# A split-precision transformer kernel whose matmul operands get other start addresses in SBUF

## The reference

```python
# first block
h = rmsnorm(x, g[0]);  proj = h @ w_in            # pool, conv, gates, q, k, v, index parts
y_pool, y_conv, y_attn = pool_mixer(..), conv_mixer(..), sparse_attention(..)
up = einsum('bsnc,ncd->bsnd', branches, w_branch)
gates = sigmoid(h @ w_gate + b_gate)
x = x + rmsnorm(sum(gates * up) @ w_out, g[1])
h = rmsnorm(x, g[2])
x = x + rmsnorm(square(relu(h @ w_up)) @ w_down, g[3])
# second block
shift, scale, gate = split(silu(c) @ w_ada + b_ada, 3)
h, hc = modulate(rmsnorm(x, norm_g), ..), modulate(rmsnorm(ctx, norm_g), ..)
p = h @ w_in_2                                    # q, k, v, z_a, u_b, z_b, g_a, g_b
attn = attention(rope(q), [rope(k), kc], [v, vc]) # kc, vc from hc @ w_in_2
y = (sigmoid(g_a) * (attn * silu(z_a)) @ w_pa + sigmoid(g_b) * (fft(u_b) * silu(z_b)) @ w_pb) @ w_o
out = rmsnorm(x + gate * y, final_g)
```

## Time and profile before

| | |
|---|---|
| median of the runs | 2207.93 us |
| span of the profiled execution | 2206.3 us |
| around the span, median less span | 1.6 us |
| TensorE busy, matmuls | 2197.4 us, 16122 instructions |
| VectorE busy | 1509.1 us |
| ScalarE busy | 1066.9 us |
| read from HBM | 468.30 MB |
| mean granted TensorE clock | 0.999 of 2.4 GHz |

### The profile page before, as it was taken

How to read it: one execution, slowest core, us unless ns; L and a number is a source line. 1 busy time by engine, 2 the same in 40 slices (tenths; PEclk the granted TensorE clock), 3 DMA queues, 4 the chain that set the end, 5 groups by cost and what they waited for, 6 DMA issues and landing times.

```text
span 2206.3 us, 37987 instructions
## 1 busy us (share of the span) xinstructions
PE 2197.4 (100%) x16122; PEld 2068.7 (94%) x16122; DVE 1509.1 (68%) x1910; ACT 1066.9 (48%) x1418; POOL 63.1 (3%) x72
## 2 busy tenths in 40 slices
PE   9999999999999999999999999999999999999998
PEld 9999999999999889989988988998889999999987
DVE  7789588888889657544554555555766656577776
ACT  5444445544444546444443543444656555444443
POOL 1000000000000000000000000000100000010001
PEclk9999999999999999999999999999999999999999
DMA  8876676788787755656656666656664445678784
GB/s 275 241 225 209 192 247 221 228 281 258 256 278 264 241 182 182 195 194 194 192 195 195 183 202 203 197 186 207 235 196 148 135 144 172 216 264 294 251 281 156
DMA packets 248034, 475.00 MB, mean 215 GB/s; under 512 B 21526, under 2 KB 26000, under 8 KB 247096
## 3 DMA queue, kind: packets, MB, share of 16 engines
q1 hardware_dynamic: 243032, 454.40, 64.7%
q0 software_dynamic: 4832, 18.16, 2.5%
HBM read 468.30 MB, written 5.78 MB: 215 GB/s over the span
## 4 chain that ended last, share of the span: by engine, by line
PE 99%; issue 0%; DVE 0%; ACT 0%; POOLq 0%; POOL 0%; DVEq 0%
PE ps L888 21%; PE ps L889 21%; PE ps L890 21%; PE ps L881 11%; PE ps L882 11%; PE ps L883 11%; PE ps L805 1%; PE ps L705 1%; PE ps L794 0%; PE ps L674 0%; PE ps L902 0%; PE ps L717 0%; PE ps L784 0%; PE ps L785 0%; PE ps L783 0%
## 5 line engine op out<-in xcount | busy, mean ns | idle before, releaser
L888 PE MATMUL ps<-op0h,whiW 128*128 128x256 f32 x3376 | 936.8, 277 | 0.0
L890 PE MATMUL ps<-op0h,wloW 128*128 128x256 f32 x3376 | 932.3, 276 | 0.0
L889 PE MATMUL ps<-op0l,whiW 128*128 128x256 f32 x3376 | 932.2, 276 | 0.0
L1279 DVE TENSOR_TENSOR wloW<-raw,whiW 128x1024 fp32r<-128x1024 f32 (+1 forms) x503 | 611.0, 1227 | 339.0 <-ACT whiW L935 336.9
L935 ACT ACTIVATE whiW<-raw 128x1024 fp32r<-128x1024 f32 (+1 forms) x504 | 529.0, 1058 | 581.1 <-PE ps L890 482.8
L888 PEld LDWEIGHTS ps<-op0h,whiW 128*128 128x128 f32 x3376 | 633.7, 188 | 2.2 <-issue 1.6
L889 PEld LDWEIGHTS ps<-op0l,whiW 128*128 128x128 f32 x3376 | 633.8, 188 | 0.5
L890 PEld LDWEIGHTS ps<-op0h,wloW 128*128 128x128 f32 x3376 | 633.7, 188 | 0.0
L1279 DVE TENSOR_TENSOR wloT<-raw,whiT 128x1024 fp32r<-128x1024 f32 (+1 forms) x264 | 317.4, 1211 | 249.5 <-ACT whiT L935 248.0
L935 ACT ACTIVATE whiT<-raw 128x1024 fp32r<-128x1024 f32 (+1 forms) x264 | 273.7, 1046 | 291.0 <-PE ps L883 243.0
L881 PE MATMUL ps<-whiT,op1h 128*128 128x512 f32 x640 | 249.2, 389 | 0.0
(11 more groups left out here) (308 smaller groups left out, 2070.2 us busy)
## 6 DMA issues: line engine op xcount, KB each, us to landing
raw<-in_w_in SPq DMA_DIRECT2D x256, 512.0 KB, 4.4
raw<-in_w_up SPq DMA_DIRECT2D x128, 512.0 KB, 3.7
raw<-in_w_down SPq DMA_DIRECT2D x128, 512.0 KB, 4.0
raw<-in_w_ada SPq DMA_DIRECT2D x96, 512.0 KB, 4.7
raw<-in_w_gate SPq DMA_DIRECT2D x96, 512.0 KB, 4.8
raw<-in_w_out SPq DMA_DIRECT2D x64, 512.0 KB, 5.1
raw<-in_w_branch SPq DMA_DIRECT2D x48, 512.0 KB, 4.9
raw<-in_w_proj_a SPq DMA_DIRECT2D x24, 512.0 KB, 5.7
```

The lines of the kernel that those rows point to most:

```text
L888: pe.matmul(o, wh, xh[:, ka, :], start=first and m % 2 == 0, stop=False, skip_group_check=True)
L889: pe.matmul(o, wh, xl[:, ka, :], start=False, stop=False, skip_group_check=True)
L890: mm = pe.matmul(o, wl, xh[:, ka, :], start=False, stop=last, skip_group_check=True)
L1279: v.tensor_tensor(wlo[job.mode][q % NSPL][:, :, 0:job.n], x, h.bitcast(F32), ALU.subtract).then_inc(s_lo, 1)
```

## The change

The places of the operands in SBUF change, and nothing else. The high part of chunk `q` begins at `PLACES[q // 4 % 16]` bytes past its buffer's base, the low part at `PLACES[(q // 4 * 3 + 5) % 16]`, in both modes; bases are 0 modulo 256 (`o - 64`). The operands x0, x1, x2, pool, conv, mix and hid0 to hid3 get tiles of their own (`placed`), which begin 0, 64, 4, 32, 32, 8, 4, 68, 64 and 12 bytes past the place where `op0h` or `op1h` begins; the low part lies 16384 bytes behind the high part. att and four stay at the start of `op1h`, and ya, ctx and mg where they are. The buffers are some bytes longer, and what is allocated after them moves up. The tmp tiles and `ident` go from 64 to 0 modulo 256 by that; `big` is put at 64 modulo 256 again. The lines where an operand's tile is written or read name the placed tile instead of `op0h`, `op0l`, `op1h`, `op1l`.

```diff
--- before.py
+++ after.py
@@ -22,6 +22,7 @@
 ATT_SCALE = 128 ** -0.5
 BIG = 1e30
 SKEW = 128 * 513 + 384
+PLACES = dict(zip("abcdefghijklmnop", (0, 64, 128, 192, 4, 68, 132, 196, 8, 72, 12, 76, 16, 32, 36, 100)))
 
 
 def constants():
@@ -291,27 +292,46 @@
             top[0] += (size + 31) // 32 * 32
             return t
 
+        def placed_at(name, k, n, off):
+
+            d = off % 32 // 4
+            return at(name, [128, k * n + 8], off - 4 * d, F32R)[:, d:d + k * n].rearrange("p (k n) -> p k n", k=k)
+
         raw = [sb(f"raw{i}", [128, KC, 512]) for i in range(NRAW)]
         def line(shift):
 
             top[0] += (shift - top[0]) % 256
             return top[0]
 
-        def split_buffers(name, stand):
+        def split_buffers(name):
 
             w = {"T": [], "W": []}
             for i in range(NSPL):
                 o = line(64)
-                for mode, shift in (("T", 0), ("W", stand)):
-                    w[mode].append(at(f"{name}{mode}{i}", [128, KC, 512], o + shift, F32R))
-                top[0] = o + stand + 4 * KC * 512
+                for mode in ("T", "W"):
+                    w[mode].append([placed_at(f"{name}{mode}{p}{i}", KC, 512, o - 64 + d) for p, d in PLACES.items()])
+                top[0] = o + 192 + 4 * KC * 512
             return w
 
-        whi, wlo = split_buffers("whi", 64), split_buffers("wlo", 192)
+        whi, wlo = split_buffers("whi"), split_buffers("wlo")
+
+        def whi_of(q):
+            return whi[chunks[q][0].mode][q % NSPL][q // NSPL % 16]
+
+        def wlo_of(q):
+            return wlo[chunks[q][0].mode][q % NSPL][(q // NSPL * 3 + 5) % 16]
+
         op0_at = line(64)
         op0h, op0l = sb("op0h", [128, 16, 256], F32R), sb("op0l", [128, 16, 256], F32R)
+        top[0] += 192
         op1_at = line(64)
         op1h, op1l = sb("op1h", [128, 16, 256], F32R), sb("op1l", [128, 16, 256], F32R)
+        top[0] += 192
+        first_of = {"x0": ("opA", op0_at), "x1": ("opB", op0_at + 64), "x2": ("opC", op0_at + 4), "pool": ("opD", op1_at + 32), "conv": ("opD", op1_at + 32),
+                    "mix": ("opE", op1_at + 8), "hid0": ("opF", op1_at + 4), "hid1": ("opG", op1_at + 68), "hid2": ("opH", op1_at + 64),
+                    "hid3": ("opI", op1_at + 12)}
+        placed = {n: (placed_at(f"{n}h", 16, 256, o), placed_at(f"{n}l", 16, 256, o + 16384)) for n, o in dict(first_of.values()).items()}
+        xhi, xlo = {x: placed[n][0] for x, (n, _) in first_of.items()}, {x: placed[n][1] for x, (n, _) in first_of.items()}
         tmp = [sb(f"tmp{i}", [128, 512]) for i in range(6)]
         ident = sb("ident", [128, 128])
         vat = sb("vat", [128, 112])
@@ -385,10 +405,8 @@
         gbc = bg("gbc", [128, 2048], 0)
         X2 = bg("X2", [128, 2, 2048], 8)
         fgb = at("fgb", [128, 2048], op1_at)
-        hi_of = {"x0": op0h, "x1": op0h, "x2": op0h, "pool": op1h, "conv": op1h, "mix": op1h, "hid0": op1h, "hid1": op1h, "hid2": op1h,
-                 "hid3": op1h, "att": op1h, "four": op1h, "ya": yah, "ctx": hch, "mg": mgh}
-        lo_of = {"x0": op0l, "x1": op0l, "x2": op0l, "pool": op1l, "conv": op1l, "mix": op1l, "hid0": op1l, "hid1": op1l, "hid2": op1l,
-                 "hid3": op1l, "att": op1l, "four": op1l, "ya": yal, "ctx": hcl, "mg": mgl}
+        hi_of = {**xhi, "att": op1h, "four": op1h, "ya": yah, "ctx": hch, "mg": mgh}
+        lo_of = {**xlo, "att": op1l, "four": op1l, "ya": yal, "ctx": hcl, "mg": mgl}
 
         columns = {}
         used = [0]
@@ -856,7 +874,7 @@
                 job, k = chunks[q]
                 banks = pair_of(job)
                 xh, xl = hi_of[job.x], lo_of[job.x]
-                h, l = whi[job.mode][q % NSPL], wlo[job.mode][q % NSPL]
+                h, l = whi_of(q), wlo_of(q)
                 if k == 0 and job.before:
                     pe.wait_ge(s_pair[job.pair], job.before)
                 elif job.name == "qi1" and k == 0:
@@ -932,7 +950,7 @@
                 act.wait_ge(s_raw[i], v)
                 if q >= NSPL:
                     act.wait_ge(s_pe, q - NSPL + 1)
-                act.activation(whi[job.mode][q % NSPL][:, :, 0:job.n], raw[i][:, :, 0:job.n], ACT.Copy).then_inc(s_hi, 1)
+                act.activation(whi_of(q)[:, :, 0:job.n], raw[i][:, :, 0:job.n], ACT.Copy).then_inc(s_hi, 1)
 
             def square(src, junk, name, tt):
                 act.activation(junk, src[:, tt, :], ACT.Square, accum_out=norm_col(name, tt)[0]).then_inc(s_sumsq, 1)
@@ -954,7 +972,7 @@
             def turn_x0(u):
                 for kt in (2 * u, 2 * u + 1):
                     act.wait_ge(s_turn0, kt + 1)
-                    act.activation(op0h[:, kt, :], bank[4 + kt % 4][:, 0:256], ACT.Identity, scale=vat[:, kt:kt + 1]).then_inc(s_x0hi, 1)
+                    act.activation(xhi["x0"][:, kt, :], bank[4 + kt % 4][:, 0:256], ACT.Identity, scale=vat[:, kt:kt + 1]).then_inc(s_x0hi, 1)
 
             def turn_x(u):
                 s, kp = u // 8, u % 8
...
@@ -1098,7 +1116,7 @@
                 for i in range(2):
                     k = 8 + 4 * job.arg + 2 * i
                     act.wait_ge(s_pair[job.pair], job.before + i + 1)
-                    act.activation(op1h[:, k:k + 2, :], half(tmp[2 + i]), ACT.Copy).then_inc(s_chi, 1)
+                    act.activation(xhi["conv"][:, k:k + 2, :], half(tmp[2 + i]), ACT.Copy).then_inc(s_chi, 1)
 
             def ep_gate(job, b0, b1):
                 n, c = job.arg
...
@@ -1270,13 +1288,13 @@
 
             def low_first(kk):
                 v.wait_ge(s_hi, 1)
-                v.tensor_tensor(wlo["W"][0][:, kk, :], raw[0][:, kk, :], whi["W"][0][:, kk, :].bitcast(F32), ALU.subtract).then_inc((s_lo0, s_lo)[kk], 1)
+                v.tensor_tensor(wlo_of(0)[:, kk, :], raw[0][:, kk, :], whi_of(0)[:, kk, :].bitcast(F32), ALU.subtract).then_inc((s_lo0, s_lo)[kk], 1)
 
             def low(q):
                 job = chunks[q][0]
-                x, h = raw[landed["w", q][0]][:, :, 0:job.n], whi[job.mode][q % NSPL][:, :, 0:job.n]
+                x, h = raw[landed["w", q][0]][:, :, 0:job.n], whi_of(q)[:, :, 0:job.n]
                 v.wait_ge(s_hi, q + 1)
-                v.tensor_tensor(wlo[job.mode][q % NSPL][:, :, 0:job.n], x, h.bitcast(F32), ALU.subtract).then_inc(s_lo, 1)
+                v.tensor_tensor(wlo_of(q)[:, :, 0:job.n], x, h.bitcast(F32), ALU.subtract).then_inc(s_lo, 1)
 
             summed = [0, 0]
 
...
@@ -1339,7 +1357,7 @@
                     low_x0(u, 1)
                     return
                 s, k = u // 8, 2 * (u % 8)
-                h, l, x = (op0h, hch)[s == 1][:, k:k + 2, :], (op0l, hcl)[s == 1][:, k:k + 2, :], half(tmp[2 + u % 2])
+                h, l, x = hi_of[ROWS[s]][:, k:k + 2, :], lo_of[ROWS[s]][:, k:k + 2, :], half(tmp[2 + u % 2])
                 if u == 8:
                     v.wait_ge(s_pe, of["b23"].end)
                 v.wait_ge(s_turned, u - 7)
```

More of the change, by code:

```diff
@@ L997, in pool_scale @@
                 act.wait_ge(s_psc, 2 * g + 2)
-                act.activation(op1h[:, 2 * g:2 * g + 2, :], half(tmp[5]), ACT.Copy).then_inc(s_phi, 1)
+                act.activation(xhi["pool"][:, 2 * g:2 * g + 2, :], half(tmp[5]), ACT.Copy).then_inc(s_phi, 1)
             def softmax1_exp(h):
@@ L1127, in ep_br @@
                     act.wait_ge(s_brm, 8 + 2 * c + i + 1)
-                    act.activation(op1h[:, k:k + 2, :], mx[:, k:k + 2, :], ACT.Copy).then_inc(s_mixh, 1)
+                    act.activation(xhi["mix"][:, k:k + 2, :], mx[:, k:k + 2, :], ACT.Copy).then_inc(s_mixh, 1)
             def ep_wo(job, b0, b1):
@@ L1153, in ep_up @@
                     act.wait_ge(s_hsq, u + 1)
-                    act.activation(op1h[:, k:k + 2, :], half(tmp[2 + u % 4]), ACT.Copy).then_inc(s_hhi, 1)
+                    act.activation(xhi[f"hid{blk}"][:, k:k + 2, :], half(tmp[2 + u % 4]), ACT.Copy).then_inc(s_hhi, 1)
             def ep_dn(job, b0, b1):
@@ L1329, in low_x0 @@
                 v.wait_ge(s_x0hi, k + 1)
-                i = v.scalar_tensor_tensor(op0l[:, k, :], bank[4 + k % 4][:, 0:256], vat[:, k:k + 1], op0h[:, k, :].bitcast(F32), ALU.mult, ALU.subtract)
+                i = v.scalar_tensor_tensor(xlo["x0"][:, k, :], bank[4 + k % 4][:, 0:256], vat[:, k:k + 1], xhi["x0"][:, k, :].bitcast(F32), ALU.mult, ALU.subtract)
                 if j:
@@ L1433, in pool_low @@
                 v.wait_ge(s_phi, g + 1)
-                v.tensor_tensor(op1l[:, 2 * g:2 * g + 2, :], half(tmp[5]), op1h[:, 2 * g:2 * g + 2, :].bitcast(F32), ALU.subtract).then_inc(s_plo, 1)
+                v.tensor_tensor(xlo["pool"][:, 2 * g:2 * g + 2, :], half(tmp[5]), xhi["pool"][:, 2 * g:2 * g + 2, :].bitcast(F32), ALU.subtract).then_inc(s_plo, 1)
             def conv_taps(b, c):
@@ L1633, in ep_cb @@
                     v.wait_ge(s_chi, 2 * blk + i + 1)
-                    v.tensor_tensor(op1l[:, k:k + 2, :], half(tmp[2 + i]), op1h[:, k:k + 2, :].bitcast(F32), ALU.subtract).then_inc(s_clo, 1)
```

(4 more changed lines are left out.)

1 line of the change is left out of this document (removed).

## The result

The changed kernel takes 2292.15 us (2292.12 and 2292.19) against 2207.93: the ratio is 1.038, with a 95% interval from 1.036 to 1.040. That is 84.2 us slower, where 27 were forecast.

What follows compares the result with a forecast made beforehand. TensorE's matmul count times pitch was taken to bound the kernel; +34.9 (W) - 10.0 (T) + 1.9 (off-16) = +26.8 us on 2206.3, plus 1.6 around the span, gave 2235 us, with an 8-in-10 range of 2175 to 2300 us.

Steps and rivals of the forecast that it cites:

- What bounds the kernel: TensorE is busy 2197.4 of 2206.3 us; time is the number of matmuls times the distance between starts.
- the surcharge: Time per matmul over bare columns at 2.4 GHz: 6.7 ns in W, 13.3 in T; read as dearer at distance 0.
- the 80 of the working: Upper bound for W (weights stationary, 256 operand columns moving): all 12048 matmuls at 120.0 ns, +80 us.
- rival 1: Places do not matter, something else separates the scores from W; 2208 us, chance 17%.
- The W term: W matmuls (weights stationary): half of the 10480 that change distance go to 120.0 ns, half stay; +34.9 us.
- The T term: T matmuls (operand stationary, weights moving): 1504 of the 3008 that move lose one 6.67 ns step; -10.0 us.
- Off-16 starts: 9320 W and T matmuls at distances off a multiple of 16 read one more line, 0.21 ns each; +1.9 us.
- Rival 2: Off-16 starts cost a whole 6.67 ns step in the six matmul lines; +71 us, 2279 us, chance 29%.
- Rival 3: Off-16 starts keep the two streams apart, so W and T get faster; -68 us, 2140 us, chance 12%.
- ScalarE, VectorE, the copy of x2, DMA: Writes at new places keep their durations and DMA is unmoved: nothing; x2 copy's possible 2.2 us only in the range.
- the forecast's own mechanism: Pitch set by weight-operand distance modulo 256, half the moved matmuls changing a step; alone 2215 to 2255 us, chance 42%.
- The sign of being wrong: Forecast is wrong if pitches leave the 6.67 ns grid, or off-16 moving operands stream several tens of ns slower.

Runs made afterwards that it cites:

- e3: Changed kernel with all operands at 64 and weights going through all sixteen high/low pairs of 0, 64, 128 and 192; 2270.26 us, 1.028 times the kernel before.
- e10: Kernel before with the weights of W also at 64, so every W and T stream stands at the same place modulo 256; 2286.24 us, 1.035 times.
- e4: Kernel before with all weights and placed operands 4 bytes further, distances between them kept; 2327.93 us, 1.054 times the kernel before.
- e1: Changed kernel's sixteen weight places, but all operands at 64 as in the kernel before; 2284.32 us, 1.0345 times the kernel before.
- e5: Kernel before with each stage's operand and weights shifted together by 8, 12, 16, 32 or 48 bytes, distances kept; 2262.75 us, run once.
- e8: Kernel before with W high parts at 0 and low parts at 128 instead of 128 and 0, T as before; 2248.05 us, 1.018 times.

## Why the prediction was right or wrong

**What bounds the kernel** was right: the change moved nothing but the distance between matmul starts, and W and T (63.1 and 20.9 us) hold the whole of it.

**That the surcharge knows addresses** was right, and so was its first reading: the 120.0 ns of the scores and of the last halves are what W takes at distance 0 (e3, e10: +78.2 us in W for the 80 of the working). The rule of the Trainium skill that was set against it (TensorE: Matmul & The Clock Gate, the phases of a matmul: two independent read ports, so that loading weights takes nothing from the running matmul) gave 2208 us, rival 1. e3, e4 and e10 each refute the 2208 us: the same instructions take 62, 120 and 78 us more by addresses alone. Whether the ports or something behind them collide, no run here shows.

**The W term failed.** I took half of the moved matmuls as unchanged, since rows showed only two distances. +34.9 us were forecast and +63.1 came. The step that failed is the assumption of one cost per distance, with even chances that a new distance costs nothing. Of sixteen pairs one is always cheap and one about half the time (e3), and the rest is not at 120.0 but mostly between 116.5 and 119.2. 12048 matmuls x (118.0 - 113.3) = 57 us by e3's average of the dear pairs, and the remainder is x2, whose start at 68 puts W near 122 ns: its matmuls take 7.8 ns more than before, those of x0 and x1 4.6. The surveys show the place of before to be the exception, and the two distances of W had been read from the exception.

**The T term had the wrong sign.** -10.0 us were forecast, from the reading that T paid one step for standing at distance 0; +20.9 came. Distance 0 for both parts is the cheapest place of T, at two steps above its columns, and every other pair costs 2 to 8 ns more (e3). At distance 0 both modes stand 13.3 ns over their columns (e10), which is W's dearest place among the multiples of 64 and T's cheapest: what W loses by leaving it says nothing of T.

**Off-16 starts** were priced at +1.9 us with a line's 0.21 ns. They cost far more: with the distances kept, 4 bytes take 7.8 ns in W and 11 in T (e4), 120 us in all. What they are worth in the change is an estimate, as the costs do not add: 22 us over what the survey of multiples of 64 takes anyway (84 less 62), of which 14 appear when the weights alone begin off 64 (e1 against e3, 2284.32 and 2270.26). No run has the pairs of the change with every start rounded to a multiple of 64. Rival 2 named the direction and nearly the time (2279), but for a cause that is by this estimate the smaller part. Its sign came in part: the x2 stages stand out, but the pair (0, 68), for one, is at 118.3 ns and not at 120.0 or more. Rival 3 is out, since nothing ran under 113.3. The line count of the Trainium skill (SBUF — State Buffer, specifications: lines of 16 bytes, a penalty for each cross) agrees in sign only: a start 16 bytes past reads no line more, and costs 4.5 ns in W and 4.4 in T (e5).

**ScalarE, VectorE, the copy of x2, DMA** were costed at nothing, and were nothing: 1062 and 422 ns as before, on the places in question. The other work of TensorE moved by 0.1 us. Nor do ScalarE's and VectorE's own accesses set the pitch: the mean W step of the changed kernel is 118.7 ns where both work, where only ScalarE does and where only VectorE does, and in e10 it is 119.9 to 120.0 in all three (worked out from the traces). What DMA writes meanwhile was not separated.

The forecast was a third of the difference and its class, within 2%, was wrong. That the range held the time was luck: it reached so far for the sake of rival 2, while the forecast's own mechanism ended at 2255. The sign of being wrong that the text named came true: pitches off the grid of 6.67 ns (117.8, 118.3, 121.1). A single matmul is no longer the period: at 117.78 ns three of them make 353.3, which is 53 times 6.67, where three at 113.33 make 51.

What stays open is the mechanism. The runs show a pitch that depends on the starts of all four streams (two weight parts, two operand parts) and for two pairs on how the stream was entered. Which accesses meet where was not seen. The records of the weight loads move with it at one place and not at another. Two groups by names (minimum, median and maximum in ns), the first before, the second in e10:

```profile
L888 PEld LDWEIGHTS ps<-op0h,whiW x3376: 186/188/192, 12.9 to 2088.7; 128*128 128x128 f32 x199
...
L911 PEld LDWEIGHTS ps<-opAh,whiWaq x3376: 186/192/193, 13.0 to 2165.7; 128*128 128x128 f32 x199
```

A load lasts 4 ns longer where every stream of W stands at one place. But T stands so too, with loads of 188 ns in both, and at (0, 128) they last 187 or 188 ns at either pitch (e8).

## What to carry to other kernels

When TensorE is the whole path and its pitch is a few per cent over the columns, the start addresses of its operands are a parameter to be surveyed, and one kernel that changes the places every few chunks measures sixteen pairs in one profile. Read such a survey chunk by chunk, not by its total and not by the median of a cell, since a cell can hold two pitches; then run the winner for the whole kernel. In a forecast, two places seen in a trace are no sample of the others; if they are the best of sixteen, every move is a loss.

## What the runs showed of the hardware

- float32r matmuls with 256 moving columns start every 113.3 to 122 ns, those with 512 every 226.7 to 240 ns, by the SBUF places of their operands alone, at an unchanged granted clock (0.999 of 2.4 GHz in every run's profile).
- With equal distances between the streams, a common shift of 32 bytes changes nothing, and 4, 8, 16 and 48 bytes cost 7.8, 6.7, 4.5 and 4.5 ns in W (e4, e5).
- Two pairs of places have two stable pitches each, 113.3 and 118.9 ns at (0, 128), 113.3 and 117.8 at (128, 128). At (0, 128) each is kept through hundreds of matmuls (e8).
- Where all streams of W stand at the same place modulo 256, a weight load is recorded with 192 ns instead of 188 and the pitch is 120.0 (e10).
- Writing float32r at 4, 8 and 12 bytes past a multiple of 16 costs ScalarE and VectorE nothing: for 1024 elements 1062 ns by ScalarE's median, 1220 to 1266 by the means of VectorE's groups, on places off 16 and on it, where before it was 1231.
